# A mixture-of-experts block: one copy of a weight block moved ahead of the result on ScalarE, and the gated tile written in natural order

## What is computed

```
for each of 64 experts e (each token picks 8 of them):
    rows  = u[tokens of e]                    # a gather
    g, p  = split(rows @ w_exp_up[e])         # 1024 -> 2 x 256
    h     = silu(g) * p                       # 256 wide
    out[tokens of e] += w * (h @ w_exp_down[e])   # 256 -> 1024, a scatter that adds
```

## Time and profile before

| | |
|---|---|
| median of 3 runs | 1233.05 us |
| the profiled execution | 1232.66 us, of which the span of the profile is 1230.4 us |
| TensorE, VectorE, ScalarE, GpSimd busy | 92%, 73%, 59%, 21% of the span |
| all experts | about from 577 us to the end |
| DMA in 600 to 1190 us | busy throughout, 360 to 376 GB/s |

### The profile page before, as it was taken

One profiled execution on the slowest core, in us unless ns is written; L12 is line 12 of the kernel. 1 busy time (PEld: TensorE's weight loads), 2 busy tenths in 40 slices (PEclk: granted clock), 3 DMA queues, 4 the chain that ended last, 5 costly groups with the idle time before them and its releaser, 6 DMA issues.

```text
span 1230.4 us, 16284 instructions
## 1 busy us (share of the span) xinstructions
PE 1135.6 (92%) x5707; PEld 856.4 (70%) x5707; DVE 902.0 (73%) x1133; ACT 724.5 (59%) x926; POOL 259.0 (21%) x145
## 2 busy tenths in 40 slices
PE   4999998988999899998999999999999999999993
PEld 3699997766777688774666666666666666666662
DVE  4575468445433586688998899999889888989881
ACT  7543342343333422513887887888778788888771
POOL 1000000000000000001233434334444434434431
PEclk9999998999999999999999999999999999999997
DMA  6413232221212233267899999999999999999972
GB/s 210 137 52 103 86 95 69 69 69 34 68 35 68 95 111 132 86 261 282 310 360 366 355 370 371 361 367 371 369 364 376 362 372 370 374 372 369 359 270 33
DMA packets 74495, 285.58 MB, mean 232 GB/s; under 512 B 10868, under 2 KB 33416, under 8 KB 49620
## 3 DMA queue, kind: packets, MB, share of 16 engines
q1 hardware_dynamic: 59716, 251.16, 54.3%
q0 software_dynamic: 14736, 33.87, 11.5%
HBM read 272.39 MB, written 29.38 MB: 245 GB/s over the span
## 4 chain that ended last, share of the span: by engine, by line
PE 53%; DMA 24%; DVE 10%; issue 6%; ACT 6%; SPq 0%; DVEq 0%; POOL 0%; ACTq 0%; POOLq 0%
PE bank L1452 43%; DMA arena<-in_w_exp_up_dram 15%; DMA out_dram<-arena 8%; ACT high L554 3%; DVE low L1356 2%; PE bank L1620 2%; PE bank L1647 2%; DVE gatheredT L1363 1%; PE bank L1531 1%; ACT arena L554 1%; PE bank L1833 1%; PE bank L1778 1%; PE bank L1632 1%; DMA arena<-in_x_dram 1%; ACT front_split L554 1%
## 5 line engine op out<-in xcount | busy, mean ns | idle before, releaser
L1356 DVE TENSOR_TENSOR low<-arena,high 128x2048 fp32r<-128x2048 f32 x192 | 436.5, 2287 | 53.6 <-ACT high L554 52.7
L554 ACT ACTIVATE high<-arena 128x2048 fp32r<-128x2048 f32 x192 | 365.2, 1918 | 30.3 <-DMA arena<-in_w_exp_up_dram 30.2
L1452 PE MATMUL bank<-high,gatheredT 128*96 128x512 f32 x1024 | 324.6, 398 | 22.7 <-DVE gatheredT L1363 22.0
L516 POOL DMA_INDIRECT arena<-u_rows,arena x64 | 136.9, 2139 | 591.1 <-DVE arena L1351 562.4
L1452 PEld LDWEIGHTS bank<-high,gatheredT 128*96 128x96 f32 x1024 | 160.2, 161 | 95.9 <-issue 26.8
L1452 PE MATMUL bank<-low,gatheredT 128*96 128x512 f32 x512 | 201.9, 394 | 0.0
L524 POOL DMA_INDIRECT out_dram<-arena x64 | 116.0, 1812 | 365.2 <-ACT arena L554 250.4
L1452 PE MATMUL bank<-high,hidT 128*96 128x512 f32 x512 | 164.7, 403 | 1.5 <-ACT arena L554 1.5
L554 ACT ACTIVATE arena<-bank 96x512 f32<-96x512 f32 (+4 forms) x217 | 107.9, 533 | 65.8 <-PE bank L1452 28.6
L1452 PE MATMUL bank<-hT_high,front_split 128*128 128x512 f32 x448 | 144.3, 404 | 0.8 <-DVE hT_low L892 0.8
L1452 PEld LDWEIGHTS bank<-low,gatheredT 128*96 128x96 f32 x512 | 82.6, 161 | 36.1
(11 more groups left out here) (253 smaller groups left out, 1402.9 us busy)
## 6 DMA issues: line engine op xcount, KB each, us to landing
arena<-in_w_exp_up_dram SPq DMA_DIRECT2D x128, 1024.0 KB, 22.9
arena<-in_w_exp_down_dram SPq DMA_DIRECT2D x64, 1024.0 KB, 19.2
arena<-in_w_in_dram SPq DMA_DIRECT2D x14, 1024.0 KB, 5.4
arena<-in_w_in_dram SPq DMA_DIRECT2D x10, 768.0 KB, 4.5
arena<-in_w_branches_dram SPq DMA_DIRECT2D x4, 1024.0 KB, 4.9
arena<-in_w_out_dram SPq DMA_DIRECT2D x4, 1024.0 KB, 5.0
arena<-in_x_dram SPq DMA_DIRECT2D x4, 512.0 KB, 5.3
arena<-in_w_mem_kv_dram SPq DMA_DIRECT2D x2, 1024.0 KB, 5.0
```

Of the source, the lines that this page charges most:

```text
L516: pool.indirect_dma_start(gathered[0:ROWS, e % 2, :], None, u_dram, bass.IndirectOffsetOnAxis(ap=index[0:ROWS, e:e + 1], axis=0), bounds_c ...
L554: return nc.scalar.activation(o, i, ACT.Copy, **kw)
L1356: v.tensor_tensor(low_part[q % SLOTS], raw[q % SLOTS], high_part[q % HIGHS].bitcast(F32), ALU.subtract).then_inc(low_done, 1)
L1452: ins = mm(bank, left[a], right[b], start=first and q == 0, stop=last and q == 2)
```

## The change

On ScalarE the high part of the first of the two next blocks is taken before `result`, not behind it. On VectorE the gated tile is written in its natural order. On TensorE the two transposes read it with a step of two elements.

```
             def expert(n, m, u, round0, start=False, last=False):      # ScalarE
...
                 copy(hidT[:, n % 2, 0, :], ps[3][:, 0:2 * ROWS]).then_inc(hidT_high, 1)
+                if blocks > 0:
+                    high(q, u + LEAD, round0)
                 if not start:
                     result(n + 1, m - 1, u + 2)
-                for j in range(min(blocks, 2)):
-                    high(q + j, u + (LEAD + j), round0)
+                if blocks > 1:
+                    high(q + 1, u + (LEAD + 1), round0)
...
             def hidden(n, m, e):                                        # VectorE
-                v.scalar_tensor_tensor(hid[0:ROWS, n % 2, :].rearrange("p (k f) -> p f k", k=2),
-                                       e_act[0:ROWS, n % 2, :].rearrange("p (f k) -> p f k", k=2), slot_w[0:ROWS, one(e)],
-                                       bank[0:ROWS, FH:2 * FH].rearrange("p (f k) -> p f k", k=2), ALU.mult,
-                                       ALU.mult).then_inc(hid_ready, 1)
+                v.scalar_tensor_tensor(hid[0:ROWS, n % 2, :], e_act[0:ROWS, n % 2, :], slot_w[0:ROWS, one(e)],
+                                       bank[0:ROWS, FH:2 * FH], ALU.mult, ALU.mult).then_inc(hid_ready, 1)
...
             def expert(n, m, u, turn, last_turn=False):                 # TensorE
-                    last = tr(ps[3][:, f * ROWS:(f + 1) * ROWS], hid[0:ROWS, n % 2, f * P:(f + 1) * P], ident[0:ROWS, 0:ROWS])
+                    last = tr(ps[3][:, f * ROWS:(f + 1) * ROWS], hid[0:ROWS, n % 2, :].rearrange("p (f k) -> p k f", k=2)[:, f, :],
+                              ident[0:ROWS, 0:ROWS])
```

## The result

| | median us | ratio to before | 95% interval |
|---|---|---|---|
| before (6 runs) | 1232.95 | | |
| changed (6 runs, 1239.76 to 1253.74) | 1242.70 | 1.0082 | 1.0046 to 1.0118 |

The forecast was 1233.0 us in 1226.5 to 1242.5. The measured time lies 0.2 us outside, on the side of the rival "the gather loop becomes the bound". The profiled execution of the changed kernel took 1253.74 us (span 1251.5), the longest of its six; its trace shows the mechanism well but its size is above the typical one. Medians and ratios leave out the two slow runs of all that were made, one of e1 at 1300.79 us (granted clock 0.843, in its other runs 0.984 to 0.987) and one of e3 at 1267.66 us.

A forecast was written before the change was run, and what follows sets the result against it. The transfer of the expert stage's bytes was taken as the bound, 9.86 us an expert. From 1232.66 us: start -0.28, end -0.28, middle 0, gather loop +0.9, giving 1233.0 us, range 1226.5 to 1242.5.

The forecast's parts named there:

- the gather loop becomes the bound: Rival: result, scatter, gather, transposes set the pace; (step - 9.86) x 58, for example 1244 or 1255 us; chance 0.17.
- The bound: Expert stage: the transfer of its bytes bounds it, mean step 9.86 us an expert; TensorE's own work is 9.40 us.
- the loop's sum: Result, scatter, gather, transposes over two experts: 17.7 us before, 19.5 with the change, 9.77 an expert, under 9.86.
- deciding point of 19.72: Length of the gather loop for two experts, in us, from which it and not the loads would be the bound.
- result to scatter: Gather loop, from the end of the result copy to the scatter: 0.28 us.
- scatter to gather: Gather loop, GpSimd's queue: scatter's median 2.05 us plus 0.30 for the step to the gather, 2.35 us.
- The +0.9 us: Allowance in the forecast sum for what the nearly closed gather loop adds by scatter, landings reaching from 9.3 to 10.6 us.
- The moved copy: ScalarE's high copy ahead of the result: `y_ready`, and the scatter and gather behind it, come 1.8 us later.
- VectorE's waits for ScalarE: VectorE gets an expert's first `high` about 1 us earlier, and its waits for ScalarE go.
- The gated tile: VectorE: 0.41 us instead of 0.69, gain 0 to 0.28; hidden in the middle, counting once at start and once at end.
- The strided weight loads: TensorE's transposes reading every second element: 0 us more for the two of an expert, at most 0.28.
- The landing of the gather: Gather loop, gather to landing: 9.9 us, plus 0.1 to the weight load; slowest landing 10.6.

The follow-up runs named there:

- e1: The kernel before with only ScalarE's order changed (one high part ahead of the result), tile as before: 1243.02 us, ratio 1.0070.
- e3: The kernel before with the result moved behind both high parts: 1257.84 us, ratio 1.0178.
- e10: e9 with the gather of expert e+4 issued ahead of the scatter of e: 1226.40 us, ratio 0.9925 to the kernel before.
- e11: e10 with one more load of 128 KB an expert: 1252.58 us, ratio 1.0132 to the kernel before.
- e12: The kernel before with the tile in natural order and the gather issued ahead of the scatter, result still copied first: 1228.99 us, ratio 0.9956.
- e2: The kernel before with only the tile's layout changed (natural order, transposes with a step of two): 1231.51 us, ratio 0.9994.
- e9: The changed kernel with odd experts' scatters going to a second tensor, so each waits for the last but one: 1245.40 us, ratio 1.0083 to the kernel before.
- e7: The kernel before with each scatter adding only the first 512 columns of its rows (2 KB instead of 4 KB): 1214.81 us, ratio 0.9850.
- e8: The changed kernel with each scatter adding only the first 512 columns of its rows: 1217.60 us, ratio 0.9882 to the kernel before.

## Why the prediction was wrong, step by step

**The bound.** Half right. The loads are the bound that remains when everything else is taken out (e10, e11, e12), and the gain for VectorE and TensorE never reached the time (e2), as forecast. But I put the whole mean step of 9.86 us down to them; e12 points to some 5 us of it as gathers and scatters already.

**The step that failed** is the loop's sum, 17.7 us before and 19.5 after for two experts, against a deciding point of 19.72. The structure and its place were right: result, scatter, gather, transposes. The sum was not:

| part | used | changed kernel, mean of some 50 experts in 660 to 1170 us |
|---|---|---|
| transposes to the end of the result | 5.1 + 1.8 = 6.9 | 7.00 |
| result to scatter | 0.28 | 0.97 |
| scatter to gather | 2.35 | 2.26 |
| gather to transposes | 9.9 + 0.1 | about 10.2 |
| sum | 19.5 (with rounding) | 20.4 |

Most of the 0.9 us is one term. I read "result to scatter" from a single expert, where the scatter went at once. In the mean of the kernel before it was already 0.70 us, since a third of its scatters (19 of 60) had been waiting for their predecessor, though only 3 of them after 860 us, where I read; in the changed kernel it is 28 of 58, and 0.97 us. That wait belongs to a loop that I had not closed: a scatter's landing, the next scatter, the gather behind it, over three experts. With 9.8 + 0.8 + 1.7 + 10.5 + 7 and the steps between it is 30.5 us in the chain, 10.2 an expert. The two loops are nearly of one length, and e9 shows that cutting the longer leaves the other: with the result to scatter back at 0.28, as I had used it, the loop of two experts still measured 20.06 us. Its terms there are scatter to gather 2.42 + 0.30 = 2.72 instead of 2.35, gather to transposes 10.06 instead of 10.0, and 7.00 from the transposes to the end of the result. So two terms were too small, and not independent of each other: a scatter that goes at once is the one that takes long to issue. The rows said so: the scatter from which I took 0.28 took 2.31 us, and I paired it with the median 2.05 over both kinds; with 2.31 the sum is 19.8, past the deciding point of 19.72. That each expert is held by whichever loop is late, so that the mean lies over either's own sum, fits these numbers but was not measured. The +0.9 us that I set aside for scatter was for one loop with a slack to 9.86, and there was none.

Its price was (step - 9.86) x 58. For e1, whose profiled execution of 1245.20 us is near the median, (10.12 - 9.86) x 58 = 15 us, less 2.4 us in start and end: 12.5, which is its whole distance to the profiled execution of the kernel before. That is bookkeeping, since the step is measured; what it says is that the whole loss lies in the steady steps, as the rival had it. The rival's chance of 0.17 was too low for a loop within 1% of the deciding point.

**The moved copy.** 1.8 us later, as forecast: from the start of the hidT copy to that of the result it was 0.23 us before (878.25 to 878.48) and 2.04 after (789.66 to 791.70), both read in the timelines. VectorE's waits for ScalarE did not go, contrary to what I wrote: in 600 to 1190 us they were 48.7 us before and 64.3 after. It gets its first block sooner and its second later, behind the result; that this is why is my reading.

**The gated tile.** 0.41 was forecast, 0.48 measured (within the 0.41 to 0.69 that I had left open); off the path (e2). **The strided weight loads.** I took 0 for both of an expert, with a bound of 0.28; it is 2 x 57 ns = 0.11 us. So the rule of the Trainium skill ("SBUF — State Buffer") that two float32 to a line of 16 bytes come at full rate does not hold for this weight load: 198 ns against 141. In the loop it is some 0.1 us; e1, which lacks it, loses as much as the changed kernel, so it decided nothing.

**The landing of the gather.** Taken as a constant. It was 10 us in both kernels and 7 in e3, which kept a worse order from costing its full price; 1 us of the difference is GpSimd's shorter issue, the rest goes with a shorter load queue.

## What to carry to other kernels

An engine that issues both the stores of results and the next loads ties them together: delaying a result by 1.8 us delayed the gather behind it, and that cost 10 us though TensorE never waits for the result itself. Before moving work ahead of such a signal, close every loop that runs through the queue, also those through a completion, and sum them from means over many rounds, with the terms of one and the same round where they depend on each other; where a loop comes within a few per cent of the bound, count it as the bound. The cure was not in the order on ScalarE but one line in the queue: issue the gather, whose condition is met earlier, ahead of the scatter.

## What the hardware showed that I had not expected

- DMA busy share is 1.02 at 369 GB/s and also at 358 GB/s in the changed kernel (860 to 1176 us); the landing of an up load there, 24.5 against 14.3 us, tells the two apart.
- A scatter of 2 KB rows lands no sooner than one of 4 KB rows (medians of 8.7 us in e7 and 8.8 in e8).
- The same scatter takes GpSimd 1.44 to 3.56 us to issue, by what VectorE does: 1.44 to 1.45 us with no split of a weight block under way at its start, and else until 1.31 to 1.37 us after the end of that split (44 of 61 scatters of the kernel before, 45 of 59 of the changed one, all 60 of e9 and all 59 of e3, where the median issue is 2.86 us). What kind of hold this is was not tried.
